# Where the small tensors lie: one address modulo 512 for all matmul operands of a decoder layer

## The reference, cut to what matters

```python
h = rms_norm(x, norm_mix); proj = h @ w_in + b_in
o_a = nsa_attention(...)          # 16 heads: compressed, selected, windowed branch
o_b = swa_sink_attention(...)     # 16 heads: window 128, sinks
x = x + jnp.concatenate([o_a, o_b], axis=-1) @ w_out
h = rms_norm(x, norm_ffn)
x = x + (jax.nn.silu(h @ w_gate) * (h @ w_up)) @ w_down
return rms_norm(x, norm_final)
```

## Time and profile before

| | us |
|---|---|
| median of 3 runs | 2134.31 |
| lowest and highest | 2134.22, 2138.91 |
| the profiled execution, its time | 2129.97 |
| the profiled execution, its span | 2128.2 |
| TensorE busy in the span | 2071.6 |
| VectorE busy | 1564.5 |
| ScalarE busy | 957.5 |
| GpSimd busy | 270.0 |

### The profile page before, as it was taken

How to read it: one execution, slowest core, us unless ns; L and a number is a source line. 1 busy time by engine, 2 the same in 40 slices (tenths; PEclk the granted TensorE clock), 3 DMA queues, 4 the chain that set the end, 5 groups by cost and what they waited for, 6 DMA issues and landing times.

```text
span 2128.2 us, 32169 instructions
## 1 busy us (share of the span) xinstructions
PE 2071.6 (97%) x13205; PEld 1827.6 (86%) x13205; DVE 1564.5 (74%) x2106; ACT 957.5 (45%) x1476; POOL 270.0 (13%) x153
## 2 busy tenths in 40 slices
PE   8999999999879999999999999999999999999998
PEld 6888777777658889999999999999999988888886
DVE  6723567767752227888889888888888888888895
ACT  5212366667652227444444444444444433333343
POOL 4000011211110000113203203203203100000001
PEclk9999999999989999999999999999999999999999
DMA  7681222221035334346445345345445765654622
GB/s 259 211 208 60 60 65 55 61 60 48 13 120 197 107 111 139 100 140 195 130 150 195 122 151 188 119 154 184 137 150 170 296 217 163 236 199 173 237 100 80
DMA packets 197779, 306.46 MB, mean 144 GB/s; under 512 B 8640, under 2 KB 121344, under 8 KB 192512
## 3 DMA queue, kind: packets, MB, share of 16 engines
q1 hardware_dynamic: 197600, 304.38, 43.3%
q10 hardware_dynamic: 32, 0.01, 0.0%
HBM read 248.79 MB, written 55.57 MB: 143 GB/s over the span
## 4 chain that ended last, share of the span: by engine, by line
PE 93%; DVE 3%; ACT 2%; issue 2%; DMA 0%; POOL 0%; DVEq 0%; ACTq 0%; POOLq 0%
PE bank L2634 12%; PE bank L2637 12%; PE bank L2639 12%; PE bank L2689 6%; PE bank L2691 6%; PE bank L2686 6%; PE bank L2235 3%; PE bank L2237 3%; PE bank L2236 3%; PE bank L2501 3%; PE bank L2503 3%; PE bank L2505 3%; PE bank L2401 3%; PE bank L2523 2%; PE bank L2525 2%; PE bank L2527 2%
## 5 line engine op out<-in xcount | busy, mean ns | idle before, releaser
L1884 DVE TENSOR_TENSOR w_all<-raw,w_all 128x1024 fp32r<-128x1024 f32 x292 | 381.3, 1318 | 82.0 <-ACT w_all L1290 81.9
L1290 ACT ACTIVATE w_all<-raw 128x1024 fp32r<-128x1024 f32 x292 | 305.7, 1058 | 299.9 <-PE bank L2691 164.5
L2639 PE MATMUL bank<-x_T,w_all 128*128 128x256 f32 x1344 | 374.9, 279 | 0.0
L2637 PE MATMUL bank<-x_T,w_all 128*128 128x256 f32 x1344 | 374.9, 279 | 0.0
L2634 PE MATMUL bank<-x_T,w_all 128*128 128x256 f32 x1344 | 374.9, 279 | 0.0
L2634 PE MATMUL bank<-x_B,w_all 128*128 128x256 f32 x1008 | 281.3, 279 | 0.5 <-DVE w_all L1884 0.5
L2639 PE MATMUL bank<-x_B,w_all 128*128 128x256 f32 x1008 | 281.2, 279 | 0.0
L2637 PE MATMUL bank<-x_B,w_all 128*128 128x256 f32 x1008 | 281.2, 279 | 0.0
L2639 PEld LDWEIGHTS bank<-x_T,w_all 128*128 128x128 f32 x1344 | 252.8, 188 | 0.0
L2634 PEld LDWEIGHTS bank<-x_T,w_all 128*128 128x128 f32 x1344 | 252.8, 188 | 0.0
L2637 PEld LDWEIGHTS bank<-x_T,w_all 128*128 128x128 f32 x1344 | 252.8, 188 | 0.0
(11 more groups left out here) (299 smaller groups left out, 4395.4 us busy)
## 6 DMA issues: line engine op xcount, KB each, us to landing
raw<-in_w_gate SPq DMA_DIRECT2D x39, 1024.0 KB, 5.2
h_scratch<-late SPq DMA_DIRECT2D x70, 512.0 KB, 3.4
raw<-in_w_down SPq DMA_DIRECT2D x50, 512.0 KB, 5.1
proj_q<-in_w_up SPq DMA_DIRECT2D x22, 1024.0 KB, 6.7
raw<-in_w_up SPq DMA_DIRECT2D x22, 1024.0 KB, 7.9
x_B<-h_scratch SPq DMA_DIRECT2D x20, 1024.0 KB, 4.9
raw<-in_w_in SPq DMA_DIRECT2D x16, 1024.0 KB, 10.2
raw<-in_w_out SPq DMA_DIRECT2D x16, 1024.0 KB, 5.2
```

Of the source, the lines that this page charges most:

```text
L1290: nc.scalar.activation(piece_hi(p), piece_raw(n, k), ACT.Copy).then_inc(piece_hi_done, 1)
L1884: nc.vector.tensor_tensor(piece_lo(p), piece_raw(n, k), piece_hi(p).bitcast(F32), ALU.subtract).then_inc(piece_lo_done, 1)
L2637: nc.tensor.matmul(dst, wl[:, t, cs], x_hi(x)[:, cols], start=False, stop=False, skip_group_check=True)
L2639: done = nc.tensor.matmul(dst, wh[:, t, cs], x_hi(x)[:, cols], start=False, stop=part == 1 and t == 3, skip_group_check=True)
```

## The change

The six small tensors, and two that were in the inner scope (`cstats`, 96 bytes, and `sink_sb`, 128 bytes), are placed ahead of `raw`. No instruction is added, removed or moved.

```diff
-        raw = sb("raw", [P, RAW, UNIT])
-        w_all = sb("w_all", [P, 2 * RING * UNIT], F32R)
         ident = sb("ident", [P, P])
         ones = sb("ones", [P, P])
         vecs = sb("vecs", [P, P])
         stats = sb("stats", [P, 4, 3, TT])
         valid = sb("valid", [P, 1])
         squares_by_row = sb("squares_by_row", [P, TT, 4])
+        cstats = sb("cstats", [P, 3, 2 * TT])
+        sink_sb = sb("sink_sb", [P, 2, SWA_HEADS])
+        raw = sb("raw", [P, RAW, UNIT])
+        w_all = sb("w_all", [P, 2 * RING * UNIT], F32R)
...
             gates = first("gates", [P, TT, N_GATES])
             kc_hi = first("kc_hi", [P, NSA_KV, 32], F32R)
             kc_lo = first("kc_lo", [P, NSA_KV, 32], F32R)
-            cstats = first("cstats", [P, 3, 2 * TT])
-            sink_sb = first("sink_sb", [P, 2, SWA_HEADS])
```

## The result

| us | before | after |
|---|---|---|
| median of 12 runs | 2132.97 | 2138.19 |
| lowest and highest | 2130.69, 2138.91 | 2134.29, 2140.04 |
| the profiled execution, its time | 2129.97 | 2137.53 |
| its span | 2128.2 | 2135.8 |

The ratio is 1.002, with a 95% interval of 1.0012 to 1.0028: slower by 0.2%. The interval leaves out 1, but the difference lies inside the 0.3% within which the prediction calls two times hard to tell apart. Behind this small number lie two large ones of opposite sign. Both kernels have the same instructions in the same order on every engine, so every difference is one of pace, of waiting or of TensorE's clock.

The account below looks back on a forecast made before the run. TensorE's pace from matmul to matmul was taken to bound the kernel. Long matmuls -21.5 us and short ones +24.8 gave +3.3 us, so the median of 2134.31 would become 2137.6 us, range 2100 to 2152.

Parts of the forecast that it names:

- Pace is everything: Dense stages: TensorE has no idle time, so only the time from matmul start to start moves the end.
- Long matmuls, 233.3 to 226.7 ns: 512 columns in input, output and down products: 3264 matmuls gain 6.6 ns each, -21.5 us.
- Rival E: Dense long streams stay at 232.2 ns while short ones take 120: +21 us, 2155.5 us; chance 0.12.
- Short matmuls, 116.67 to 120 ns: 256 columns in gate and up and the first products: 7440 matmuls lose 3.33 ns each, +24.8 us.
- Rival C: Short matmuls stay near 116.7 ns (115 to 118) and only long ones gain: 2113 us; chance 0.17.
- Rival B: Short matmuls settle at 113.3 ns as the long ones settle: -46 us, 2088 us; chance 0.14.
- Rival D: Place makes no difference in dense stages, or tensors don't lie as their names say: 2134 us; chance 0.07.
- The rest costs nothing: VectorE's sums and DMA transfers at new places taken as nothing; unhidden, thirty sums by 8 ns would be 0.2 us.
- The granted clock doesn't change: Expected of the profile after: idle time and TensorE's granted clock stay as before; no term in the sum.
- The side remark: Operands 0 apart modulo 512 seemed to cost the same per loaded stationary tile, 13.3 or 13.4 ns, whatever moves.
- The range: 2100 to 2152 us, said to leave out Rival B and the tip of Rival E, less than 0.2.

Follow-up runs that it names:

- e5_after_again: The changed kernel, unchanged, measured once more: 2136.45 us, ratio 1.0014 to the kernel before.
- e8_distance256: The changed kernel with 256 bytes of small tensors placed between `w_all` and the other operands: 2137.07 us, ratio 1.0027 to the kernel before.
- e1_bench: A kernel without the computation: blocks of 60 float32r matmuls with nothing else running, operand distances swept mainly in steps of 32 bytes; 815.9 us.
- e7_up112: The changed kernel with the moving operands of gate and up read 112 bytes further on: 2095.77 us, ratio 0.9834 to the kernel before.
- e6_bench2: The matmul bench of e1_bench again, with distances in steps of 8 bytes, bfloat16 and float32 operands, and one repeated stationary tile: 1118.49 us.

## Why the prediction was right

Forecast 2137.6 us, measured 2138.19. That the two numbers lie 0.6 us apart is luck: the median of before was 2134.31 when I predicted and 2132.97 over 12 runs, and the clock moved three stages by some 4 us that the sum doesn't have. The differences tell more: +3.3 us forecast; +5.2 by these medians, +2.0 in e5_after_again, +5.2 in e8_distance256, whose distances are equal to those of after modulo 256. What was right is the mechanism and both of its terms.

- **Pace is everything.** Right for the dense stages. TensorE is without idle time in the same windows, and the counts moved as forecast: 5000 for 5002, and 1493 long ones in 338 us where 1501 in 340 were forecast, which is 1492 in 338.
- **Long matmuls, 233.3 to 226.7 ns.** Right. At equal clock the stages give input -4.9 (5.4 by 816 x 6.6 ns), output -4.6 (5.1), down -11.1 (11.1), together -20.6 against -21.5; the -22.4 of the two profiles holds 1.8 us of the clock. Rival E, that a dense stream stays at 232.2, fell: the unsettled start is real, but at most ten steps long in e1_bench.
- **Short matmuls, 116.67 to 120 ns.** Right, and this was the choice that carried the risk: gate and up +23.0 us (7056 x 3.33 = 23.5), the first products +1.2 at equal clock (1.3), together +24.2 against +24.8. The runs of eight scores were a fair sample, since a short stream at distance 0 is at 120 from its third or fourth step (e1_bench); at 112 bytes, where it takes ten, they would not have been. Rival C fell with the same number.
- **Rival B**, 113.3 ns, fell at this distance but not as a pace: it exists, at 112 bytes, and e7_up112 takes it. I had looked for it on the wrong axis, in how long a stream runs, when it was a matter of where the operands lie.
- **Rival D** fell: e1_bench shows both pairs of paces with nothing else running. The Trainium skill's two independent read ports ("TensorE: Matmul & The Clock Gate", "Part 2: What happens when you issue a matmul") agree with the bfloat16 blocks of e6_bench2, at 215.9 ns whatever the distance, and don't account for float32r.
- **The rest costs nothing.** Right for VectorE and for DMA: VectorE does the same work at 496.54 of 600 and 303.63 of 340 us and holds nothing up; at 89% of the down stage, as forecast.
- **"The granted clock doesn't change"** was wrong outside the dense stages. The time at 1.2 GHz went from 37.0 to 45.9 us in the profiled executions: -1.8 us in the input, +1.5 in the first products, +4.5 in the attention, which I had taken as unchanged. The sum had no term for it.
- **The side remark**, that being equal costs 13.3 ns for each loaded tile, fits 128 stationary columns and fails with fewer (e1_bench). Nothing in the sum rested on it but the comfort that it gave to 120.
- **The range.** I wrote that it holds most of rival E, but E's own price, 2155.5, lies above its end at 2152. With B, chances of up to 0.26 stood outside, not less than 0.2.

What stays open: why the distance matters. The runs show a period of 256 bytes, float32r only, no dependence on the absolute place or on other engines, and an effect even when the stationary tile stays the same (120.00 and 117.77 ns). What inside TensorE makes the distance count isn't shown, nor why 8 bytes gave two values, why fewer stationary columns help a short stream at distance 0 and not a long one, and why 104 and 112 bytes stand at opposite ends.

## What to carry to other kernels

Where TensorE has no idle time, read its pace from start to start for each shape, and look for matmuls of the same shape elsewhere in the same trace that run at another pace: they forecast what a move of operands does, with its sign. One address for all operands was a trade between two lengths of matmul; float32r streams are better placed each for itself, with the moving operand's address the stationary one's modulo 256 for 512 moving columns, and 112 bytes further on for 256, which took 1.7% off this kernel where the uniform placement cost 0.2%. A change that moves the total by 0.2% can hold two terms of 1%: split it by stage before calling it nothing, and compare stages at equal clock, since a stretch of 3.4 us at 1.2 GHz moved a stage by 1.5 to 2.3 us here. The direction counts too: 112 bytes gave 113.37 ns with 256 columns, and 144, which is -112, gave 116.70.

## What the runs showed of the hardware

- A float32r matmul's pace depends on the distance of its two operands modulo 256 bytes: 226.67 to 240 ns with 512 columns, 113.37 to 130.03 with 256 (e1_bench, e6_bench2). The best values, 226.67 and the 113.33 that e7_up112 settles at, are 17/16 of the 213.33 and 106.67 ns of one column a cycle at 2.4 GHz; why isn't shown.
- A short stream's best distance isn't a long one's: at 0 those of 512 columns are at their best and those of 256 slower than at 288 (120.00 against 116.67); with 384 and 448 columns 0 is better than 288 (173.33 against 176.73, 202.67 against 204.43), and with 128, 192 and 320 these two are alike.
- Below 256 columns a float32r matmul with a stationary tile of 128 columns of its own gets hardly faster than the 113.37 ns of the best 256: 111.67 ns with 128 columns, 111.73 with 192.
- A float32r stream needs up to ten matmuls after a start to come to its pace (none to ten at distance 0 with 512 columns, e1_bench), and ten after each wait in e7_up112; a short wait thus costs more than its own length.
- With the same instructions TensorE's granted clock was at the 1.2 GHz level for 37.0 us of one execution (before) and 49.2 of another (e5_after_again). In the attention 27.3 us at that level went with 404.8 us, 34.1 and more with 408.7 to 409.4.
